# A decoder-layer step: the modulation weight loaded by blocks of 128 rows instead of 256 columns, first-norm tokens modulated after their transpose

## What is computed

```python
sh1, sc1, g1, sh2, sc2, g2 = split(silu(c) @ w_ada + b_ada, 6)   # c: 1 + 8 rows, w_ada: 1024 x 6144
h    = rmsnorm(x, norm1_g) * (1 + sc1) + sh1
proj = h @ w_in                       # 1024 x 3072: q, k, v of 12 heads, u, gate_b, gate_c
attn, states = dilated window attention (3 groups x 4 heads), with per-head q/k norm and bias
conv = gate_b * short_conv(gate_c * u)
x    = x + g1 * (concat(attn, conv) @ w_o)
h2   = rmsnorm(x, norm2_g) * (1 + sc2) + sh2
x    = x + g2 * (top-8 of 64 experts(h2) + shared expert(h2))
```

## Time and profile before

| | |
|---|---|
| runs | 1299.69, 1302.67, 1302.62 us; median 1302.62 |
| profiled execution | 1304.99 us; its span 1303.1 us |
| busy share of the span | PE 86%, DVE 37%, POOL 20%, ACT 16% |
| granted TensorE clock, mean | 0.947 |
| moved by DMA | 370.99 MB |

### The profile page before, as it was taken

How to read it: one execution, slowest core, us unless ns; L and a number is a source line. 1 busy time by engine, 2 the same in 40 slices (tenths; PEclk the granted TensorE clock), 3 DMA queues, 4 the chain that set the end, 5 groups by cost and what they waited for, 6 DMA issues and landing times.

```text
span 1303.1 us, 17147 instructions
## 1 busy us (share of the span) xinstructions
PE 1119.3 (86%) x6061; PEld 551.4 (42%) x6061; DVE 482.7 (37%) x1081; ACT 211.5 (16%) x464; POOL 260.3 (20%) x282
## 2 busy tenths in 40 slices
PE   5899775887999999698999998998989989899880
PEld 1355442444577756554333333333333333333330
DVE  3455576543245644723222221232212222122225
ACT  1421111000133301302111111011111111111110
POOL 1000222210212040001232331222212222222321
PEclk9999888988979999899999999999999989999995
DMA  9874678664767286319799999999999999999946
GB/s 306 272 254 148 219 236 281 185 153 119 218 211 197 76 311 265 117 41 409 267 392 374 388 375 373 381 390 383 364 368 375 380 381 343 374 380 368 385 105 221
DMA packets 103169, 370.99 MB, mean 285 GB/s; under 512 B 13334, under 2 KB 52779, under 8 KB 78000
## 3 DMA queue, kind: packets, MB, share of 16 engines
q1 hardware_dynamic: 69128, 258.84, 50.8%
q0 software_dynamic: 26368, 79.49, 22.9%
q10 hardware_dynamic: 7636, 32.17, 7.1%
HBM read 342.84 MB, written 66.02 MB: 314 GB/s over the span
## 4 chain that ended last, share of the span: by engine, by line
PE 46%; DMA 39%; DVE 6%; SPq 3%; issue 3%; ACT 1%; POOL 0%; DVEq 0%; ACTq 0%; POOLq 0%
DMA mem<-in_w_up_e 29%; PE pb L1501 14%; DMA mem<-in_w_ada 8%; PE pb L1206 7%; PE pb L1360 4%; PE pb L1521 3%; PE pb L1210 2%; PE pb L1438 2%; PE pb L1116 2%; PE pb L1093 2%; PE pb L1338 2%; SPq L580 1%; PE pb L1281 1%; PE pb L1294 1%; SPq L612 1%
## 5 line engine op out<-in xcount | busy, mean ns | idle before, releaser
L1501 PE MATMUL pb<-mem 128*32 128x512 f32 (+2 forms) x1792 | 352.4, 607 | 25.7 <-DMA mem<-in_w_up_e 25.1
L1501 PEld LDWEIGHTS pb<-mem 128*32 128x32 f32 (+2 forms) x1792 | 120.1, 131 | 244.2 <-issue 243.4
L1521 PE MATMUL pb<-mem 128*32 128x512 f32 (+2 forms) x896 | 177.4, 597 | 2.6 <-issue 2.6
L1990 DVE SCALAR_TENSOR_TENSOR mem<-pb,mem 128x256 f32<-128x256 f32 x48 | 32.4, 676 | 320.7 <-ACT mem L1063 253.3
L1093 PE MATMUL pb<-mem 128*128 128x128 f32 (+3 forms) x644 | 96.2, 287 | 59.3 <-ACT mem L1050 26.6
L1206 PE MATMUL pb<-mem 128*128 128x384 f32 x384 | 136.1, 511 | 0.0
L779 POOL DMA_INDIRECT y_d<-mem x48 | 69.7, 1453 | 299.6 <-DVE mem L1996 159.5
L1093 PEld LDWEIGHTS pb<-mem 128*128 128x128 f32 (+3 forms) x644 | 74.1, 148 | 110.9 <-issue 58.7
L1206 PEld LDWEIGHTS pb<-mem 128*128 128x128 f32 x384 | 74.9, 200 | 57.2 <-issue 14.2
L1521 PEld LDWEIGHTS pb<-mem 128*32 128x32 f32 (+2 forms) x896 | 57.0, 129 | 97.8 <-issue 97.8
L774 POOL DMA_INDIRECT mem<-h_d,mem x54 | 61.0, 1130 | 184.9 <-issue 140.7
(11 more groups left out here) (256 smaller groups left out, 1059.5 us busy)
## 6 DMA issues: line engine op xcount, KB each, us to landing
mem<-in_w_gate_e SPq DMA_DIRECT2D x64, 1024.0 KB, 17.5
mem<-in_w_up_e SPq DMA_DIRECT2D x64, 1024.0 KB, 26.1
mem<-in_w_down_e SPq DMA_DIRECT2D x64, 1024.0 KB, 23.2
mem<-in_w_ada SPq DMA_DIRECT2D x24, 1024.0 KB
mem<-in_w_in SPq DMA_DIRECT2D x8, 1536.0 KB
mem<-new_d POOLq DMA_DIRECT2D x16, 512.0 KB, 6.7
out<-in_cache_k_w ACTq DMA_DIRECT2D x8, 1020.0 KB, 7.3
out<-in_cache_v_w ACTq DMA_DIRECT2D x8, 1020.0 KB, 21.3
```

The source lines that it names most:

```text
L1501: mm = eng.matmul(pb[t % 2][lo:hi, :].rearrange("p (q f) -> p q f", q=2), lhsT=xT[t][:, k, lo:hi], rhs=wgu[c][:, :, k, :], start=(k == 0), ...
L1521: mm = eng.matmul(pb[2 + half][lo:hi, :], lhsT=he[t][:, f, lo:hi], rhs=wdn[c][:, f, 512 * half:512 * half + 512], start=(f == 0), stop=(f ...
```

## The change

`w_ada` is loaded in 24 blocks of 128 rows by 2048 columns (1 MB each, rows of 8 KB). Blocks 0 to 7 together make sh1 and sc1, 8 to 15 g1 and sh2, 16 to 23 sc2 and g2. A block is four matmuls of 512 columns in four column strips, which add up over eight blocks in one bank; the bias is put into the bank by four matmuls ahead of the first block. Blocks 0 to 7 have slots of their own; later blocks alternate between slots 2 and 9. The tokens and constants are loaded ahead of all weights. The tokens are normed in one pass without modulation, turned between the blocks, and scaled and shifted in `hT`, where the channel is the partition and scale and shift are columns (`scT`, `shT`). The bias vectors are made ahead of that. The eight first cache copies are issued behind the modulation.

```diff
-ADA_W = 256
-ADA_N = SEC // ADA_W
-ADA_1 = 2 * D // ADA_W
+ADA_W = 2048
+ADA_R = SEC // ADA_W
+ADA_C = ADA_W // 512
...
 def ring_items():
-    items = [("ada", i) for i in range(ADA_1)]
-    slots = [0, 1, 3, 4, 5, 2, 3, 4]
+    items = [("ada", k) for k in range(KD)]
+    slots = [7, 3, 4, 5, 6, 8, 2, 1]
...
     for c in range(chunks):
+        items += [("ada", KD + 2 * c), ("ada", KD + 2 * c + 1)]
+        slots += [2, 9]
         if c + 1 < chunks:
             items += [("proj", c + 1)]
             slots += [(c + 1) % 2]
-        items += [("ada", ADA_1 + 2 * c), ("ada", ADA_1 + 2 * c + 1)]
-        slots += [2, 2]
...
         @block.sync
+            eng.dma_start(rows8[:], a["norm1_g"].rearrange("z (k p) -> (z k) p", p=P)).then_inc(s_in, 16)
+            eng.dma_start(b_rows[:], b_ada).then_inc(s_in, 16)
+            eng.dma_start(cst[:], a["k_cst"]).then_inc(s_cst, 16)
+            for r in range(DIL):
+                eng.dma_start(x_t[:, r, :], xp[r]).then_inc(s_x, 16)
+            eng.dma_start(x_t[0:NS, SAMPLE, :], xs).then_inc(s_x, 16)
...
                     if k0 == "ada":
-                        eng.wait_ge(s_mrow, i0 + 1)
+                        eng.wait_ge(s_ada, i0 + 1)
...
         @block.gpsimd
...
+                if n == 16:
+                    eng.wait_ge(s_msb, 6)
+                    mods_out(1)
+            eng.wait_ge(s_m1, 7)
+            mods_out(2)
...
         @block.scalar
...
+            eng.wait_ge(s_ada, KD)
+            eng.activation(msb[:], pb[4][:, :], ACT.Copy).then_inc(s_msb, 1)
+            eng.wait_ge(s_m1, 1)
+            eng.wait_ge(s_hT, 2 * TILES)
+            for k in range(1, KD, 2):
+                eng.activation(hT[:, k, 0:SEQ], hT[:, k, 0:SEQ], ACT.Identity, bias=shT[:, k, 0:1],
+                               scale=scT[:, k, 0:1]).then_inc(s_msb, 1)
+            for copy in copies[0:FIRST_COPIES]:
+                eng.dma_start(*copy).then_inc(s_caches, 16)
...
         @block.tensor
             def ada(i):
...
+                r, k = i // KD, i % KD
+                bank = pb[4 + r % 2]
+                if k == 0:
+                    for c in range(ADA_C):
+                        q = ADA_C * r + c
+                        eng.matmul(bank[32 * c:32 * c + 32, :], lhsT=ident[0:SEC // 512, q:q + 1].to_broadcast([SEC // 512, 32]),
+                                   rhs=b_rows[:, :], start=True, stop=False)
                 ring_in(n)
...
+                for c in range(ADA_C):
+                    mm = eng.matmul(bank[32 * c:32 * c + 32, :], lhsT=cT[:, k, :], rhs=ring[slots_of[n]][:, 512 * c:512 * c + 512],
+                                    start=False, stop=(k == KD - 1))
+                mm.then_inc(s_ada, 1)
...
+            for k in range(1, KD):
+                ada(k)
+                if k <= TILES:
+                    first_turn(k - 1)
+            eng.wait_ge(s_msb, 1)
+            for j in range(4):
+                mm = turn(pb[5][:, P * j:P * (j + 1)], msb[:, P * j:P * (j + 1)], P)
+            mm.then_inc(s_hTp, 1)
...
         @block.vector
...
+            link(eng.tensor_tensor(samples, samples, by_sample(scT), ALU.mult))
+            eng.tensor_tensor(samples, samples, by_sample(shT), ALU.add).then_inc(s_m1, 1)
+            eng.wait_ge(s_hT, 2 * TILES)
+            for k in range(0, KD, 2):
+                eng.tensor_scalar(hT[:, k, 0:SEQ], hT[:, k, 0:SEQ], scT[:, k, 0:1], shT[:, k, 0:1], ALU.mult, ALU.add
+                                  ).then_inc(s_m1, 1)
...
-                    if j - 1 in ada_after(c):
-                        ada_evac(ADA_1 + 2 * c + ada_after(c).index(j - 1))
...
+            eng.wait_ge(s_ada, ADA_R * KD)
+            eng.wait_ge(s_tables, 16 * 9)
+            eng.wait_ge(s_modw, 16 * ADA_C)
+            eng.tensor_copy(msb[64:128, :], pb[4][64:128, :])
+            eng.scalar_tensor_tensor(out=msb[0:64, :], in0=pb[4][0:64, :], scalar=1.0, in1=gn2, op0=ALU.add, op1=ALU.mult
+                                     ).then_inc(s_m1, 1)
```

More of the change, by code:

```diff
@@ L147, in constants @@
     put("iotacol", i[:, None])
[L149 to L153, removed]
     ohp = np.zeros((33, NVEC, VL), np.float32)
@@ L347, in build @@
         m2 = [[at(m_smp + D * (3 * s + i), D) for i in range(3)] for s in range(2)]
-        h_row = [at(m_att + D * i, D) for i in range(2)]
+        xn = [at(m_kn, D), at(m_smp + 5632, D)]
+        junk1 = at(m_kn, D)
         junk = at(m_att + 2 * D, D)
@@ L354, in build @@
         bv = at(m_qk, NVEC * VL, parts=G * H)
[L355 removed]
+        bs = at(m_hT, T * SW, parts=G * H)
+        b_rows = at(m_att + 2560, 512, parts=SEC // 512)
         upP = at(m_cv, 2, 2 + SEQ)
@@ L369, in build @@
         rows19 = at(m_vr + P, CC, parts=19)
+        rows8 = at(m_vr + P + CC, P, parts=KD)
         t19 = tensor(2, 19)
@@ L385, in build @@
         snm, szs, srz = (small[:, 60 + i:61 + i] for i in range(3))
-        h2_row = h_row
+        h2_row = [at(m_att + D * i, D) for i in range(2)]
         sg = at(m_cv, 2, NTOK)
@@ L433, in build @@
         s_cst, s_tables, s_in, s_x = sem("s_cst"), sem("s_tables"), sem("s_in"), sem("s_x")
-        s_ring = [sem(f"s_ring{i}") for i in range(2 * RING)]
+        s_ring = [sem(f"s_ring{i}") for i in range(len(ring))]
         s_set, s_csig, s_cs = sem("s_set"), sem("s_csig"), sem("s_cs")
@@ L437, in build @@
         s_bmm, s_bev, s_bvw, s_ts = sem("s_bmm"), sem("s_bev"), sem("s_bvw"), sem("s_ts")
-        s_ada, s_mrow, s_each = sem("s_ada"), sem("s_mrow"), sem("s_each")
-        s_modw = [sem(f"s_modw{i}") for i in range(4)]
+        s_ada, s_msb, s_modw = sem("s_ada"), sem("s_msb"), sem("s_modw")
         s_g1 = sem("s_g1")
@@ L690, in _ @@
             eng.wait_ge(s_ts, 1)
-            for i in range(ADA_1, ADA_1 + 4):
-                mod_out(i)
+            eng.wait_ge(s_ada, KD)
+            for c in range(2):
+                eng.dma_start(gn2[32 * c:32 * c + 32, :], a["norm2_g"][:, 512 * c:512 * c + 512].to_broadcast([32, 512])
+                              ).then_inc(s_tables, 16)
             eng.wait_ge(s_qout, 32)
@@ L742, in _ @@
             eng.wait_ge(s_spv, SPV[-1])
-            for i in range(4):
-                eng.wait_ge(s_modw[i], 16 * ((ADA_N - ADA_1) // 4))
+            eng.wait_ge(s_modw, 2 * 16 * ADA_C)
             for i, sec in ((0, 2), (1, 4), (2, 3)):
@@ L871, in _ @@
                                    ACT.Copy).then_inc(s_bev, 1)
-            for copy in copies[0:FIRST_COPIES]:
-                eng.dma_start(*copy).then_inc(s_caches, 16)
+            eng.wait_ge(s_x, 16 * TILES)
+            for j in range(TILES):
+                if j:
+                    eng.wait_ge(s_ss1, j)
+                eng.activation(junk1[0:nt(j), :], x_t[0:nt(j), j, :], ACT.Square,
+                               accum_out=ss1[0:nt(j), j:j + 1]).then_inc(s_ss1, 1)
+            eng.wait_ge(s_var1, 2)
+            eng.activation(rs1, ss1, ACT.Sqrt).then_inc(s_sd1, 1)
             for j, tt in enumerate(ORDER):
@@ L908, in _ @@
                         whole = part
+                    if z == 20:
+                        eng.wait_ge(s_ada, 2 * KD)
+                        eng.activation(msb[:], pb[5][:, :], ACT.Copy).then_inc(s_msb, 1)
                     if z < 20:
@@ L1158, in _, with first_turn @@
             mm.then_inc(s_bmm, 1)
-            for j, tt in enumerate(ORDER):
+            def first_turn(j):
+                tt = ORDER[j]
                 n = nt(tt)
```

167 lines of the change are left out of this document (55 added, 112 removed).

## The result

The changed kernel takes 1241.54 us (median of four runs, 1241.4 to 1246.7), the kernel before on the same chip 1301.61: a ratio of 0.955 (0.953 to 0.958), 60 us less. The forecast was 1237.6, range 1222 to 1260. The profiled execution took 1241.44 us, its span is 1239.6, the mean granted clock 0.957.

The account below looks back on a forecast made before the run. Among what the change touches, it saw PE held by late `in_w_ada` loads, the slow clock behind them and the stretch before the projections. Its terms summed to −65.0 us: 1240.0 from the profiled 1304.99, 1237.6 on the median; range 1222 to 1260.

Parts of the forecast that it names:

- Stops and their clock: Projection chunks: all seven PE stops for `in_w_ada` go, −42.7 us, and the slow clock behind them, −12.9.
- Bias matmuls: Modulation: three new groups of four matmuls put in the bias, two of them in the chunks: +2.0 us.
- DVE's fewer instructions: Projection chunks: DVE loses four or five small instructions for each piece of `in_w_ada`, counted as 0.
- ACT: Start of the projections: issuing eight cache copies just ahead of the first Square delays the first `kn`, +1.5 us (0 to 3).
- The front: Stretch before the chunks: ends at 53.5 us in place of 74.42, −20.9, with ends −18 and −27; PE mostly at 1.2 GHz.
- End of the projections: Hand-over to the attention: bias tables queue behind the last row block's evacuation and POOL's stores, +5.0 us (2 to 7).
- Transfers: Chunks, mainly 3 and 4: the same bytes must move in less time, +3 us in the sum.
- Score loads starve: Chunks 3 and 4: each 1 MB score load lets one row block pass, 21 us come back: 1258 us; chance 0.14.
- Long front: Before the chunks: slow block loads keep the first unit near 74 us, total 1258; chance 0.08.
- Late blocks: Chunks: row blocks take longer than a chunk to land, PE stops at all 16, slower than before; chance 0.04.
- More than forecast: Front and hand-over: PE at 2.4 GHz from 25 us and tables in time, 1226 us; chance 0.07.
- the signs that were to show it: First unit at 50 to 56 us, no later `in_w_ada` wait, clock 1.00 through chunks of about 228 us, `bias_d` wait.

Follow-up runs that it names:

- the lead alone: Kernel before, old 256-column pieces, with a second slot and, from the second chunk on, pieces requested ahead of `in_w_in`: 1247.6 us, ratio 0.961.
- spread copies: Eight cache copies issued one behind each of units 6 to 13: on the changed kernel 1234.9 us, on the kernel before with early piece requests 1249.4.
- the store by POOL: Changed kernel with the two sample-query stores (`new_d`, 48 KB) on POOL's queue instead of ACT's: 1232.9 us, ratio 0.947.
- the old order: Changed kernel with each chunk's `in_w_in` requested ahead of its two row blocks: 1256.2 us with one shared slot, 1257.3 with two.
- the kernel with early copies: Changed kernel with the eight cache copies issued right behind the bias vectors, ahead of the first norm's squares: 1247.2 us, ratio 0.958.
- the three kernels without the lead: Changed kernel with later blocks sharing one slot and requested after `in_w_in` (1256.2 us), two slots but requested after it (1257.3), one slot but ahead (1251.8).
- the best version: Changed kernel with cache copies behind units 6 to 13, last blocks evacuated between DVE's two products, and bias tables issued early: 1223.2 us, ratio 0.940.

## Why the prediction was right, and where its steps were off

- *Stops and their clock* (−42.7 and −12.9). Right, and for the reason given: the request a chunk ahead. With the lead alone the old chunks lost 58.2 us, 2.6 more than the two terms together. Of that 2.4 is the first unit, at the slow level before (2.79 and 6.54 us) and at the fast one with the lead alone (1.50 and 5.43): the forecast counted no clock there, and the lead doesn't explain it, since with its lead the changed kernel has a slow first unit too (2.49 and 6.08).
- *Bias matmuls* (+2.0): two groups of 1.06 us in the time line of the changed kernel, at 57.64 and 185.16, and 1.9 by the difference of 222.1 and 220.2 (both with spread copies). *DVE's fewer instructions* (0): nothing to be seen either, by the same pair.
- *ACT: "The issue of eight cache copies ... delays the first `kn`: +1.5 (0 to 3)"*. This is the step that failed: the copies cost the chunks 13.6 to 15.0. I counted the issue alone, and took DVE's sum for its cover. The cover was too short (1.02 us of wait, 2.37 in the store by POOL), and the main cost was not in the issue at all but in what stands behind the copies on that queue: a 48 KB store that lands 27.31 us after its issue and for which DVE must wait before it writes the first of its three `kn` buffers again. A step that is moved takes its transfers along; I named the queue, but not who needs the next entry in it.
- *The front* (−20.9): −26.6, near the end of −27 that I had allowed. The step that failed is "so I stay near the slow end": PE was at the faster level from 37.83 us on, not only in the chunks. The other parts held: L1139 (before L1156) ended at 29.1, forecast 29.3. That the copies had to leave for it, and that they cost 16 us there otherwise, was no part of the working.
- *End of the projections* (+5.0): +5.9, by the mechanism forecast; the landing of the first table was the part that took longer.
- *Transfers* (+3, 0 to 15): about 0 at PE. DVE waited 17.8 us for the sample queries of the scores, 4.2 at the longest, yet PE waited for DVE at L1089 only 5.5 us in all, about 1 us more than in the earlier trace rows, and 1.02 of that is the wait behind the copies; the units of lead covered it.
- The rivals. *Score loads starve*: half of it happened. With 1 KB runs and the same lead DVE waited 5.8 us for these loads, with rows of 8 KB 16 to 20 in four kernels that differ in where copies and stores go. That is the direction of the rule of the Trainium skill ("DMA: Bandwidth & Descriptors", "Queues, rings and completion order") that queues take turns by packets; that the packets are the cause was not tried by itself. The order of requests counts too: with rows of 8 KB in the old order it was 10.0 and 10.7 us. PE did not pay for it. (The trace of before does have rows of 8 KB, in the expert loads, but no score loads beside them.) *Long front*: fell, but the kernel with early copies shows it at 63.7. *Late blocks*: fell; `in_w_ada` landed 10.0 us after issue in the median of all 24 blocks, with a chunk of lead for the later ones. It is what the three kernels without the lead show in a smaller size. *More than forecast*: the best version reaches 1223, by removing the two losses that the changed kernel has.

Of the signs that were to show it, three did not come: the first unit starts earlier than 50 us, the clock does not stay at 1.00 through the chunks, and these last 237 us and not 228.

So the forecast of −65 was met by −60 while one of its small terms was nine to ten times too small; the surplus of the front and of the stops, and transfers that cost PE nothing, paid for most of it. That the total came out so close is luck.

## To carry to other kernels

When stops at a load are seen, look at when the request goes out before changing what is loaded: a second slot and another order in the list of loads gave the old kernel 52 us, where the whole change gave 60. When transfers are moved to another place in a program, list what stands behind them on that queue and who waits for its landing, since here a store of 48 KB landed only behind the 8 MB ahead of it. Where a last step feeds nothing soon, put it behind the loads that the next stage needs.

## What was unexpected of the hardware

- A store of 48 KB took 27.31 us behind eight copies of 1 MB on one queue, and 6.5 us on another queue while the engines moved as much (413 against 405 GB/s, 60 to 75 us).
- In the front the profile shows a granted clock of 1.00 (the columns of the windows above), from 20 to 45 us in the changed kernel and from 20 to 75 in the one before, and yet in the changed kernel a block took 1.94 us until 37.8 us and 1.06 afterwards. There the level is read from the durations, not from that column.

```profile
30.00:35.00 5.00, 4.80 (x29) 2.06 (x22) 2.34 (x4) 0.71 (x3) 0.00 (x0) 1.00 1.01 421
```

- Code that no kernel changed, from the shared expert's last product to the end, took 709.6 to 717.6 us in thirteen profiled executions, one of each kernel. Whether that is chance or follows from what goes before is not shown. A gain of 5 us ahead of it is seen in its stage and can be missing from the total.
